# A hybrid encoder in fp32: where the last recurrence step meets the output projection's first products

## The reference

```python
def step(state, inp):
    r_t, w_t, k_t, v_t, kk_t, a_t = inp
    sa = jnp.einsum('bhvk,bhk->bhv', state, -kk_t)
    state = (state * w_t[:, :, None, :] + sa[..., None] * (kk_t * a_t)[:, :, None, :]
             + v_t[..., None] * k_t[:, :, None, :])
    y = jnp.einsum('bhvk,bhk->bhv', state, r_t)
    return state, y
...
mu_y = jnp.mean(y, axis=-1, keepdims=True)
var_y = jnp.mean(jnp.square(y - mu_y), axis=-1, keepdims=True)
y = (y - mu_y) * lax.rsqrt(var_y + GN_EPS)
y = y * gn_g + gn_b
y = y + jnp.sum(rh * kh * r_k, axis=-1, keepdims=True) * vh
y = y.reshape(B, S, D) * g
return y @ w_o
...
h = h + g_m * y
```

## Time and profile before

| | |
|---|---|
| time, median of 3 runs | 2922.53 us (2917.65 to 2927.41) |
| time of the profiled execution | 2923.66 us |
| span of its profile | 2921.9 us |
| TensorE busy | 2796.2 us, 96% |
| VectorE / ScalarE / GpSimd busy | 1968.7 / 1371.6 / 1436.0 us |
| last pair's chain | 2113.76 to about 2125.2 us of the span |
| projection's first product, its m = 2 begins | 2125.97, 2158.70 us |

### The profile page before, as it was taken

How to read it: one execution, slowest core, us unless ns; L and a number is a source line. 1 busy time by engine, 2 the same in 40 slices (tenths; PEclk the granted TensorE clock), 3 DMA queues, 4 the chain that set the end, 5 groups by cost and what they waited for, 6 DMA issues and landing times.

```text
span 2921.9 us, 63562 instructions
## 1 busy us (share of the span) xinstructions
PE 2796.2 (96%) x25936; PEld 2220.0 (76%) x25936; DVE 1968.7 (67%) x2812; ACT 1371.6 (47%) x2295; POOL 1436.0 (49%) x961
## 2 busy tenths in 40 slices
PE   8899899999999999999999999999989999999998
PEld 6544567877888888876678788878867788888887
DVE  6687887688777777787034166766647766655667
ACT  5476977244333334436334256555424444334445
POOL 0001000334777677774356455655363576667772
PEclk9899999999999999999999999999999999999999
DMA  8100000622323233221533311221122112111111
GB/s 303 69 1 15 1 2 1 245 65 83 99 72 100 72 90 97 77 96 43 202 116 115 124 60 53 76 82 47 49 93 58 44 44 59 56 43 57 50 51 73
DMA packets 194397, 225.29 MB, mean 77 GB/s; under 512 B 14862, under 2 KB 151649, under 8 KB 194209
## 3 DMA queue, kind: packets, MB, share of 16 engines
q1 hardware_dynamic: 182529, 180.66, 19.9%
q10 hardware_dynamic: 11680, 42.01, 3.9%
HBM read 185.15 MB, written 37.22 MB: 76 GB/s over the span
## 4 chain that ended last, share of the span: by engine, by line
PE 72%; DVE 9%; issue 3%; ACT 3%; POOL 2%; DMA 1%; SPq 0%; ACTq 0%; DVEq 0%; POOLq 0%
PE ps L148 18%; PE ps L150 18%; PE ps L149 18%; PE ps L3827 3%; PE ps L3836 2%; PE ps L2294 2%; PE ps L2283 1%; DVE uc L1080 1%; PE ps L2305 1%; PE ps L3756 1%; PE ps L3834 1%; POOL w_lo L727 1%; ACT d_r L2436 1%; DVE d_r L2696 1%; PE ps L3771 1%
## 5 line engine op out<-in xcount | busy, mean ns | idle before, releaser
L148 PE MATMUL ps<-x_hi,w_hi 128*128 128x512 f32 x1160 | 454.4, 392 | 5.2 <-POOL w_lo L727 5.2
L150 PE MATMUL ps<-x_hi,w_lo 128*128 128x512 f32 x1160 | 452.0, 390 | 0.0
L149 PE MATMUL ps<-x_lo,w_hi 128*128 128x512 f32 x1160 | 451.9, 390 | 0.0
L727 POOL TENSOR_TENSOR w_lo<-w_room,w_hi 128x512 fp32r<-128x512 f32 x188 | 291.9, 1565 | 227.4 <-ACT w_hi L1242 227.4
L727 POOL TENSOR_TENSOR w_lo<-sq_room,w_hi 128x512 fp32r<-128x512 f32 x182 | 281.8, 1559 | 225.8 <-ACT w_hi L1242 225.8
L1080 DVE SCALAR_TENSOR_TENSOR uc<-u,pc,uc 128x1024 f32<-128x1024 f32 x176 | 319.5, 1826 | 21.8 <-ACT uc L1256 11.5
L1068 DVE TENSOR_TENSOR u<-u,ps 128x512 f32<-128x512 f32 x228 | 151.3, 684 | 195.8 <-PE ps L150 171.4
L148 PEld LDWEIGHTS ps<-x_hi,w_hi 128*128 128x128 f32 x1160 | 218.1, 188 | 54.0 <-POOL w_lo L727 6.5
L150 PEld LDWEIGHTS ps<-x_hi,w_lo 128*128 128x128 f32 x1160 | 218.0, 188 | 45.9
L149 PEld LDWEIGHTS ps<-x_lo,w_hi 128*128 128x128 f32 x1160 | 218.2, 188 | 44.7
L148 PE MATMUL ps<-g_hi,w_hi 128*128 128x512 f32 x640 | 249.3, 390 | 0.7 <-DVE h L1146 0.5
(11 more groups left out here) (490 smaller groups left out, 6921.4 us busy)
## 6 DMA issues: line engine op xcount, KB each, us to landing
w_room<-in_f_w_up_dram SPq DMA_DIRECT2D x48, 512.0 KB, 5.0
rwkv_scratch<-rp_stage ACTq DMA_DIRECT2D x48, 512.0 KB, 3.5
sq_room<-in_f_w_up_dram SPq DMA_DIRECT2D x40, 512.0 KB, 4.6
ada_w<-in_ada_w_dram SPq DMA_DIRECT2D x80, 256.0 KB, 2.8
rc_raw<-rwkv_scratch SPq DMA_DIRECT2D x28, 512.0 KB, 4.2
d_ada_w<-in_ada_w_dram SPq DMA_DIRECT2D x24, 512.0 KB, 7.8
d_r<-in_ada_w_dram ACTq DMA_DIRECT2D x24, 512.0 KB, 6.6
sq_room<-in_f_w_down_dram SPq DMA_DIRECT2D x24, 512.0 KB, 4.3
```

What stands on the lines that cost most here:

```text
L148: pe.matmul(out, w_hi, x_hi, start=first, stop=False, skip_group_check=skip)
L149: pe.matmul(out, w_hi, x_lo, start=False, stop=False, skip_group_check=skip)
L150: return pe.matmul(out, w_lo, x_hi, start=False, stop=last, skip_group_check=skip)
L727: pool.tensor_tensor(slot_of(k.w_lo, s), src, slot_of(k.w_hi, s).bitcast(F32), ALU.subtract).then_inc(w_lo_done, 1)
```

## The change

It moves and splits work around the last pair's chain.

- SyncE: pair 6's store and pair 7's gate fetch leave the pair loop. The list now reads: gain weights of pair 7, weight blocks 0 and 1, stored tiles kt 0 to 5, store of pair 6's y, gate fetch of pair 7, stored tile kt 6.
- Buffers: the fetched tiles and the high and low parts get places (class `Rows`, `y_t(kt)`) over buffers of pair 7 that are free early; waits are set accordingly.
- GpSimd: `lows_pool` works ahead of block 2 (n == 2), not ahead of block 1.
- TensorE: behind each chain step e = 1 to 15 comes one of three passes of one kt of m = 0, in both halves (`out_third`), so kt 0 to 4 are done within the chain. Then m = 0 kt 5 and 6, m = 1 kt 0 to 3, `back_pe(7)`, m = 1 kt 4 and 5, m = 0 kt 7, m = 1 kt 6 and 7.
- Pair 7's gating, high and low parts are done in two halves of 512 tokens on VectorE, ScalarE and VectorE.

```diff
+class Rows:
+    def __init__(self, room, places):
+        self.room, self.places = room, places
+    def __getitem__(self, at):
+        return self.room[at[0], self.places[at[1]], at[2]]
...
-    y_t = st.enter_context(nc.sbuf_tensor("rc_y_t", [P, KT, S], F32))
-    y_hi = st.enter_context(nc.sbuf_tensor("rc_y_hi", [P, KT, S], F32R))
-    y_lo = st.enter_context(nc.sbuf_tensor("rc_y_lo", [P, KT, S], F32R))
-    nsq = st.enter_context(nc.sbuf_tensor("rc_nsq", [P, 3, S], F32))
+    y_front = st.enter_context(nc.sbuf_tensor("rc_y_front", [P, KT, S], F32))
+    y_split = st.enter_context(nc.sbuf_tensor("rc_y_split", [P, 2 * KT, S], F32R))
+    y_rest = st.enter_context(nc.sbuf_tensor("rc_y_rest", [P, 2, S], F32))
...
+    def y_t(kt):
+        return y_front[:, kt, :] if kt < 5 else y_rest[:, kt - 5, :]
+    y_hi = Rows(y_split, (12, 14, 9, 2, 3, 4, 5, 6))
+    y_lo = Rows(y_split, (13, 15, 7, 8, 10, 11, 1, 0))
...
             if p:
                 load_gn(p)
-                store(p - 1)
-            sp.dma_start(g_in[:, :], scr[G_, p, :, :]).then_inc(sem["g_ld"], 16)
+            if p + 1 < PAIRS:
+                if p:
+                    store(sp, p - 1)
+                load_g(sp, p)
...
         for e in range(STEPS):
             chain_pe(pe, PAIRS - 1, e)
-        for kt in range(KT - 1):
+            if e:
+                out_third(pe, 0, (e - 1) // 3, (e - 1) % 3)
+        for kt in range(5, KT - 1):
             out_pe(pe, 0, kt)
-        for kt in range(3):
+        for kt in range(4):
             out_pe(pe, 1, kt)
         back_pe(pe, PAIRS - 1)
-        for kt in range(3, KT - 2):
+        for kt in range(4, KT - 2):
             out_pe(pe, 1, kt)
...
+    def out_third(pe, m, kt, part):
+        if part == 0:
+            wait_split(k, pe, b0 + m, kt)
+            pe.wait_ge(lo_done, kt + 1)
+        w, y = (k.w_hi, k.w_hi, k.w_lo)[part][m][:, kt, :], (y_hi, y_lo, y_hi)[part]
+        for n in range(NH):
+            cols = halves(n)
+            pe.matmul(k.ps[m][:, cols], w, y[:, kt, cols], start=kt == part == 0, stop=False, skip_group_check=True)
...
         if kt < KT - 1:
             pe.wait_ge(lo_done, kt + 1)
-        else:
-            pe.wait_ge(lo_last, 1)
         for n in range(NH):
+            if kt == KT - 1:
+                pe.wait_ge(lo_last, n + 1)
...
-        act.wait_ge(sem["bv"], PAIRS)
-        act.wait_ge(sem["q_ps"], 2 * PAIRS)
+        act.wait_ge(sem["bt"], PAIRS)
+        act.wait_ge(sem["g2_ps"], BLK * PAIRS)
+        act.wait_ge(sem["g3_ps"], BLK * PAIRS)
         for kt in range(KT - 1):
             act.wait_ge(y_back[kt], 16)
-            high_act(act, kt, y_t[:, kt, :])
+            if kt == 3:
+                act.wait_ge(sem["q_ps"], 2 * PAIRS - 1)
+                act.wait_ge(sem["ks_sb"], 6 * PAIRS)
+            act.activation(y_hi[:, kt, :], y_t(kt), ACT.Copy).then_inc(hi_done, 1)
...
+        for i in range(2):
+            act.wait_ge(sem["y"], PAIRS + i)
+            act.activation(y_hi[:, KT - 1, halves(i)], g_in[:, halves(i)], ACT.Copy).then_inc(hi_done, 1)
...
-        gate_dve(dve, PAIRS - 1)
-        dve.wait_ge(hi_done, KT)
-        dve.wait_ge(sem["y"], PAIRS)
-        dve.tensor_tensor(y_lo[:, KT - 1, :], g_in[:, :], y_hi[:, KT - 1, :].bitcast(F32), ALU.subtract).then_inc(lo_last, 1)
+        dve.wait_ge(sem["tp"], PAIRS)
+        dve.wait_ge(sem["g_ld"], PAIRS * 16)
+        for i in range(2):
+            dve.scalar_tensor_tensor(out=g_in[:, halves(i)], in0=k.ps[3][:, halves(i)], scalar=col("b_gn_b", PAIRS - 1),
+                                     in1=g_in[:, halves(i)], op0=ALU.add, op1=ALU.mult).then_inc(sem["y"], 1)
+        for i in range(2):
+            dve.wait_ge(hi_done, KT + i)
+            dve.wait_ge(sem["y"], PAIRS + i)
+            dve.tensor_tensor(y_lo[:, KT - 1, halves(i)], g_in[:, halves(i)], y_hi[:, KT - 1, halves(i)].bitcast(F32), ALU.subtract
+                              ).then_inc(lo_last, 1)
...
         if n == 2:
-            sp.wait_ge(sem["q_sb"], 4 * PAIRS)
-            sp.wait_ge(sem["q_ps"], 2 * PAIRS)
-            for kt in range(KT - 1):
-                sp.dma_start(y_t[:, kt, :], yscr[kt, :, :]).then_inc(y_back[kt], 16)
+            sp.wait_ge(sem["bt"], PAIRS)
+            sp.wait_ge(sem["bon_ps"], PAIRS)
+            sp.wait_ge(sem["pend"], PAIRS)
+            for kt in range(KT - 2):
+                back(kt)
+            store(sp, PAIRS - 2)
+            load_g(sp, PAIRS - 1)
+            back(KT - 2)
...
     def lows_pool(pool, n):
-        if n == 1:
+        if n == 2:
             for kt in range(KT - 1):
                 pool.wait_ge(hi_done, kt + 1)
-                pool.tensor_tensor(y_lo[:, kt, :], y_t[:, kt, :], y_hi[:, kt, :].bitcast(F32), ALU.subtract
+                if kt == 2:
+                    pool.wait_ge(sem["q_ps"], 2 * PAIRS - 1)
+                    pool.wait_ge(sem["ks_sb"], 6 * PAIRS)
+                if kt == KT - 2:
+                    pool.wait_ge(sem["q_ps"], 2 * PAIRS)
+                pool.tensor_tensor(y_lo[:, kt, :], y_t(kt), y_hi[:, kt, :].bitcast(F32), ALU.subtract
                                    ).then_inc(lo_done, 1)
```

More of the change, by code:

```diff
@@ L3462, in loads_pair0, with store, load_g @@
         load_r(sp, 0)
+    def store(sp, p):
+        sp.wait_ge(sem["y"], p + 1)
+        sp.dma_start(yscr[p, :, :], g_in[:, :]).then_inc(sem["store"], 16)
+        sp.wait_ge(sem["store"], 16 * (p + 1))
+    def load_g(sp, p):
+        sp.dma_start(g_in[:, :], scr[G_, p, :, :]).then_inc(sem["g_ld"], 16)
     def sp_part(sp):
@@ L3471, in load_gn @@
             sp.dma_start(gng, a.b_gn_g[0:1, p * P:(p + 1) * P].to_broadcast([P, P])).then_inc(sem["gn_ld"], 16)
[L3473 to L3476, removed]
         pair0.values_stored(sp)
@@ L4074, in out_pe @@
             pe.wait_ge(lo_done, kt + 1)
-        else:
-            pe.wait_ge(lo_last, 1)
         for n in range(NH):
+            if kt == KT - 1:
+                pe.wait_ge(lo_last, n + 1)
             cols = halves(n)
             last = passes3(pe, k.ps[m][:, cols], k.w_hi[m][:, kt, :], k.w_lo[m][:, kt, :], y_hi[:, kt, cols], y_lo[:, kt, cols],
-                           kt == 0, kt == KT - 1)
+                           kt == 0, kt == KT - 1, True)
         if kt == KT - 1:
@@ L4265, in loads_sp, with back @@
     def loads_sp(sp, i, n):
+        def back(kt):
+            sp.dma_start(y_t(kt), yscr[kt, :, :]).then_inc(y_back[kt], 16)
         if n == 0:
```

## The result

The changed kernel takes 2931.73 us (median of 12 runs, 2923.53 to 2937.06) against 2922.08 (12 runs, 2911.60 to 2928.78): a ratio of 1.0027, 95% interval 1.0015 to 1.0039, which is about 8 us slower (the medians lie 9.7 apart). It is a small change, but the interval lies clear of 1. Forecast were 2918 and a range of 2910.5 to 2926. The profiled execution's span is 2930.0 us, 8.1 longer than before, and m = 2, my yardstick, begins at 2166.94 instead of 2158.70, 8.2 later. So the whole difference lies ahead of m = 2 (0.6 us of it ahead of the changed part), and nothing is given back behind it.

A forecast was written before the change was run, and what follows sets the result against it. TensorE was taken to bound the kernel, with 72% of the chain of waits. +3.8 on the chain, -6.95 in the normalisation and -1.4 behind the transposes gave -4.6 us: a median of 2918 us, range 2910.5 to 2926.

The forecast's parts named there:

- my yardstick: Start of m = 2, after which both programs do the same work; forecast at 2154.1 against 2158.7, -4.6 us.
- the weights are issued behind the gain weights: SyncE's list: weights fetched from about 2102.1, 10.0 us earlier than before, not in the levels.
- block 0 lands: Weight block 0 ready for GpSimd 5.5 us after its issue, at 2107.6 (2106.1 to 2109.9).
- the stop behind step 1: TensorE, after chain step 1, waits some 5.3 us, 2114.1 to 2119.4, for GpSimd's low part of kt 0.
- the normalisation: From `y_act` to the transposes: 12.1 us instead of 19.05, -6.95, as GpSimd is idle meanwhile.
- The clock: Pair 7's chain: the stop brings the low clock for 4.4 us, then full clock; `y_act` at 2134.2, 3.8 us later.
- rival (c): Chain at low clock to its end: `y_act` at 2141.6, m = 2 at 2161.5, 2925.3 us; chance 0.08.
- a further stall: An added delay which, together with the chain at low clock throughout, was needed for a slower result; chance 0.05.
- my sum: Section to m = 2: +3.8 on the chain, -6.95 in the normalisation, -1.4 behind the transposes, -4.6 us in all.
- Behind the transposes: TensorE from the transposes to m = 2: six matmuls fewer there, -1.4 us.
- rival (a): Second low clock from 3.4 us idle before the transposes, costing 1.8 to 2.7 us: 2920.3 us; chance 0.20.
- The step at low clock: Chain step with two products on TensorE: 1.55 us at the low clock, 0.90 at full clock.

The follow-up runs named there:

- best: single, with GpSimd splitting blocks 0 and 1 in its idle time within pair 7's levels, ahead of pair 6's gain: 2909.60 us, ratio 0.9951 to the kernel before.
- no_stop: Changed kernel with weights and stored tiles fetched before pair 7's gain weights, and low parts made between the splits of blocks 0 and 1: ratio 0.9984 to the kernel before.
- bare: Changed kernel with the products of m = 0 moved out of the chain to behind it, all else as changed: ratio 0.9984 to the kernel before.
- single: no_stop with one product of m = 0 behind each chain step in place of two: 2912.59 us, ratio 0.9969 to the kernel before.
- dense: Changed kernel with four products behind each chain step, for m = 0 and m = 1: one run, section 61.69 us against 57.03 before the change.
- warm: Changed kernel with eight extra fp32 matmuls, result never read, behind chain step 1: one run, section 57.69 us against 57.03 before the change.
- lows_only: Changed kernel with the low parts made between the splits of blocks 0 and 1, fetches as changed: ratio 1.0004 to the kernel before.
- fetch_only: Changed kernel with weights and stored tiles fetched before pair 7's gain weights, GpSimd's order as changed: ratio 1.0012 to the kernel before.

## Why the prediction was wrong

Right, point by point: the weights are issued behind the gain weights and not in the levels; block 0 lands 5.7 us after its issue (5.5 forecast); the stop behind step 1 is there, released by the low part of kt 0, though only 2.16 us of it show as such, since step 1 itself came late; the normalisation shrinks to 12.2 us (2145.32 to 2157.51) from 19.1, for the reason given, where I had 12.1 (the 19.05 that the sum starts from is 19.03 by its own rows). best has 12.2 too. no_stop has 12.9, bare 13.95 to the end of `gain` and single 14.2, since there work of GpSimd still stands beside the first operations.

Wrong is the step "The clock". I let the low clock hold 4.4 us and paid 1.9 us for it. It held 34 us, the whole chain, and the 14.3 steps took 24.7 us (2120.66 to 2145.32) instead of 14.8. I had taken the length from two rows in which what follows is products alone, and put it in front of a mixture without any row for it. The argument "with products there is no idle time" against rival (c) was the error in the reasoning: TensorE was busy without a gap and the clock didn't come back. What came was rival (c) with a further stall, the case to which I had given 0.05. no_stop against the changed kernel shows that what stands before the chain matters, for the same mixture stays at 1.00; dense shows that the kind of work matters, for with four products a step the clock came back. So it did in bare, after the small matmuls of `tail_pe` and step 1.

By terms, against my sum: `y_act` 14.9 us later instead of 3.8. Of these, 4.1 are the late step 1 (0.6 drift, 2.2 more without instructions than the 0.86 of before, 1.2 because the last matmuls of `tail_pe` run at 0.50, 2.82 us for 1.61), which I had not priced at all, only named as something that would show me wrong; the rest is the chain, 27.5 us from step 1 to `y_act` where I had 20.4. Of the 7.1 more, the steps are 9.9, and the wait behind step 1 was 2.8 shorter than forecast (2.85 from step 1 to the release instead of 5.6). The normalisation gave its 6.9. Behind the transposes I had -1.4 and it was +0.2: the second low stretch of rival (a) ate it. Together 14.9 - 6.9 + 0.2 = 8.2.

The step at low clock was mis-sized too: 1.77 us, not 1.55. With 1.77 rival (c) would have read 2119.4 + 25.3 = 2144.7 for `y_act` and +5.9 for the section. At full clock it is 1.04, not 0.90. That is 0.45 + 0.455 + 0.14, and 0.14 us that I had not put in. The single product shows about as much (0.45 + 0.23 would still have fitted into 0.72, it took 0.81: 0.13 more than the sum). A cost of changing between small and wide matmuls would explain both; no run takes it apart.

The missing instructions: they go with the density of the transfers. The DMA share between 2108 and 2112 is 1.01 in the changed kernel. Where the transfers stand as there (changed, warm, dense, lows_only, bare), 3.07 to 3.56 us pass without instructions. In the kernel before the share there is 0.32, and in it and in the four kernels whose early fetches have ended by then (no_stop, fetch_only, single, best) 0.86 us pass. The traces also show the transfers of a DMA queue that they call "instruction", one of 16 KB every few us. In the kernel before, the one that belongs to this place starts between 2109.5 and 2110.0, 1.2 to 1.7 us before TensorE runs dry (2111.19). In the changed kernel it starts between 2112.5 and 2113.0, 0.7 to 1.2 us after TensorE has run dry (2111.81), and TensorE goes on 1.9 to 2.6 us after it in both. warm, dense, lows_only and bare have it late too, 0.3 to 1.4 us after, and no_stop, fetch_only, single and best early, 1.2 to 2.0 us before. So dense transfers go with a late transfer of instructions in these profiles. What holds it up, queueing in the same engines or something else, wasn't tried, and the queue's name doesn't say whose instructions they are.

What stays open: why 3.07 us lose the clock in some executions and not in the profiled one of warm. The length of the wait alone doesn't tell. Waits of 2.15 us (changed) and 2.21 us (single) ahead of the transposes were followed by the low clock, those of 2.95 and 3.07 us (warm) were not, and in bare the clock came back 3.4 us after it had fallen. So the changed kernel's runs may well hold both cases. Its twelve runs have a mean granted clock of 0.977 to 0.984, the 19 runs of the kernel before that were timed beside no_stop 0.982 to 0.987; eight of the changed kernel's runs lie below 0.982 and four don't. With one profile each it can't be told for a single run.

## What to carry to other kernels

Before putting wide matmuls into the gaps of a serial chain, ask at which clock the chain will start: in every profile here the mixture of two products a step kept the clock that it found, 1.04 us a step or 1.77. Waits ahead of it, of 3.1 to 3.8 us here, can set that clock, though not in every execution. One product where the gap holds one is nearly free (0.09 us a step), and in the two profiles that have it the clock stayed at 1.00 through the chain. If TensorE's next work needs another engine's result, look at that engine's whole list in order: here moving two splits into 12 us of idle time of GpSimd was worth 3.6 us of section, while one product a step in place of two was worth 2.0.

## What the runs showed of the hardware that was not expected

TensorE was granted 0.50 for 24 us in which the profile counts it busy in every microsecond (the three rows from 2122 to 2146 above). The Trainium skill, "TensorE: Matmul & The Clock Gate", section "What's actually happening", says that recent activity of the array releases the throttle; the trace agrees only if one doesn't take the profile's busy time for that activity: with two products a step the clock stayed low, with four it came back. The same section's default state, throttled until work releases it, is what the changed kernel's chain looks like.

Two engines in each other's way: with GpSimd's low parts alongside, a VectorE pass took 3.30 us, without 1.22. In bare the tiny operation just before the first pass was drawn out to 1.98 us, from 0.17, until GpSimd's last low part was done, and the pass itself took 1.23. So what GpSimd's work costs VectorE can stand in the duration of a small operation ahead of the pass, and the pass itself looks untouched.
